# Key compression, its branch and the stick heads' projections become lanes of the attention region

## What is computed

```python
for i in range(DEPTH):                       # DEPTH = 2
    hn = rmsnorm(h, ln_mix[i])
    (g_q, g_k, g_v, g_z, g_a, g_b, n_q, n_kc, n_vc, n_ks, n_vs, n_kw, n_vw, n_gate,
     s_q, s_k, s_v) = jnp.split(hn @ w_in[i], SPLIT_POINTS, axis=-1)
    o_gdn = gated_deltanet(g_q, g_k, g_v, g_z, g_a, g_b, ...)
    o_nsa = native_sparse_attention(n_q, n_kc, n_vc, n_ks, n_vs, n_kw, n_vw, n_gate, ...)
    o_sb = stick_breaking_attention(s_q, s_k, s_v)
    mix = jnp.concatenate([o_gdn, head_rmsnorm(o_nsa), head_rmsnorm(o_sb)], axis=-1)
    h = h + mix @ w_out[i]
    ...

def compress(kv, pe, w1, w2):                # key compression: 31 blocks of 32 tokens, stride 16
    blocks = kv[:, idx] + pe[None, None, :, None, :]
    return jax.nn.silu(blocks.reshape(b, n_cmp, g, CMP_LEN * d) @ w1) @ w2

# in native_sparse_attention: three branches, each a softmax and a product, gated and added
p_c = masked_softmax(q @ kc, ...);  o_c = p_c @ vc          # the compressed branch
out = gate0 * o_c + gate1 * o_s + gate2 * o_w               # selected and window branches
```

## Time and profile before

| | us |
|---|---|
| median of 3 runs | 4019.28 |
| lowest and highest | 4017.68 and 4022.88 |
| the profiled execution | 4020.51 |
| its span | 4018.7 |

### The profile page before, as it was taken

How to read it: one execution, slowest core, us unless ns; L and a number is a source line. 1 busy time by engine, 2 the same in 40 slices (tenths; PEclk the granted TensorE clock), 3 DMA queues, 4 the chain that set the end, 5 groups by cost and what they waited for, 6 DMA issues and landing times. The chain is left out here.

```text
span 4018.7 us, 46953 instructions
## 1 busy us (share of the span) xinstructions
PE 3640.0 (91%) x19533; PEld 2787.1 (69%) x19533; DVE 1795.1 (45%) x2763; ACT 1312.1 (33%) x2028; POOL 423.9 (11%) x347
## 2 busy tenths in 40 slices
PE   5989888999998899998897979999989978799998
PEld 4777756888685668876675537788766654477885
DVE  4775556433324343325442434454454424345534
ACT  3332453222323332324222433333342124333423
POOL 0002001210001012000230000310002300003100
PEclk7999999999998899998996959999999969699999
DMA  6641324522220212303100011323131000123230
GB/s 227 205 147 37 87 69 139 173 94 90 84 79 16 104 66 94 112 32 112 40 12 23 1 54 62 110 85 116 37 98 39 12 22 1 68 74 105 78 119 23
DMA packets 230400, 316.19 MB, mean 79 GB/s; under 512 B 13085, under 2 KB 169606, under 8 KB 228910
## 3 DMA queue, kind: packets, MB, share of 16 engines
q1 hardware_dynamic: 230190, 313.20, 23.7%
HBM read 310.52 MB, written 6.85 MB: 79 GB/s over the span
## 5 line engine op out<-in xcount | busy, mean ns | idle before, releaser
L493 PE MATMUL out<-h_lo,w_hi 128*128 128x512 f32 x2608 | 1043.3, 400 | 43.9 <-DVE w_lo L484 39.7
L484 DVE TENSOR_TENSOR w_lo<-ring,w_hi 128x1024 fp32r<-128x1024 f32 (+2 forms) x473 | 582.3, 1237 | 993.8 <-ACT w_hi L479 988.9
L494 PE MATMUL out<-h_hi,w_hi 128*128 128x512 f32 x2608 | 1022.5, 392 | 0.0
L495 PE MATMUL out<-h_hi,w_lo 128*128 128x512 f32 x2608 | 1022.3, 392 | 0.0
L479 ACT ACTIVATE w_hi<-ring 128x1024 fp32r<-128x1024 f32 (+2 forms) x473 | 483.3, 1028 | 1172.4 <-PE out L495 1078.7
L493 PEld LDWEIGHTS out<-h_lo,w_hi 128*128 128x128 f32 x2608 | 494.2, 189 | 168.1 <-issue 51.0
L494 PEld LDWEIGHTS out<-h_hi,w_hi 128*128 128x128 f32 x2608 | 494.1, 189 | 112.4 <-issue 11.0
L495 PEld LDWEIGHTS out<-h_hi,w_lo 128*128 128x128 f32 x2608 | 493.8, 189 | 104.2
L493 PE MATMUL item_banks<-h_lo,w_hi 128*128 128x512 f32 (+1 forms) x696 | 317.5, 456 | 14.4 <-DVE w_lo L484 5.1
L495 PE MATMUL item_banks<-h_hi,w_lo 128*128 128x512 f32 (+1 forms) x696 | 279.4, 401 | 0.0
L494 PE MATMUL item_banks<-h_hi,w_hi 128*128 128x512 f32 (+1 forms) x696 | 279.2, 401 | 0.0
(11 more groups left out here) (487 smaller groups left out, 4654.8 us busy)
## 6 DMA issues: line engine op xcount, KB each, us to landing
ring<-in_mlp_w SPq DMA_DIRECT2D x30, 2048.0 KB, 8.7
ring<-in_w_up SPq DMA_DIRECT2D x44, 1024.0 KB, 6.5
tiles<-in_mod_w SPq DMA_DIRECT2D x80, 512.0 KB, 4.5
ring<-in_e_w_in SPq DMA_DIRECT2D x48, 512.0 KB, 4.2
ring<-in_w_in SPq DMA_DIRECT2D x22, 1024.0 KB, 5.3
ring<-in_w_down SPq DMA_DIRECT2D x10, 2048.0 KB, 7.8
ring<-in_o_w_in SPq DMA_DIRECT2D x7, 2048.0 KB, 7.9
tiles<-in_mod_w SPq DMA_DIRECT2D x8, 1024.0 KB, 8.7
```

What stands on the lines that cost most here:

```text
L484: return nc.vector.tensor_tensor(lo.bitcast(F32R), x, hi, ALU.subtract)
L493: nc.tensor.matmul(out, wh, xl, start=start, stop=False, **kw)
L494: nc.tensor.matmul(out, wh, xh, start=False, stop=False, **kw)
L495: return nc.tensor.matmul(out, wl, xh, start=False, stop=stop, **kw)
```

## The change

Three things move in each layer, and nothing that is computed changes.

- `compress_keys` and its block with its barrier go. `compress_lane` does the same work in the attention region. Its position term no longer has 32 matmuls of its own: POOL copies the vectors behind the token pairs, so that each of the 32 matmuls has 65 columns and the last column is that term. The tokens of the odd blocks between the two groups come out too and are left unused. The pairs lie in the sparse and stick tiles of `mixT`, which are empty by then.
- The compressed branch leaves the sparse lane and becomes `compressed_lane`, in the PSUM bank `stick_out`. It writes its result to `mixT` by ACT, and the sparse lane adds its own to that (`leave`). The sparse lane keeps its 48 steps in their order.
- The six items of the stick heads leave the mixing region (23 are left there) and run as an `items_lane` of the attention region, in `stick_banks`. The ring and `w1` share their memory with the stick lane's tiles, so the stick lane starts behind them. `h_hi` and `h_lo` are kept for it.

In planned times the six items take 4 to 73, the stick heads 75 to 157, the norms 159 to 208, and the sparse lane 2 to 198. In the mixing region an item beside the delta lane is planned at 9.4 where it had 8.6, and the rotary lane begins behind the last item.

```diff
-def compress_keys(k, a, l, k2, v2, kc_dup, vc_rows):
...
+def compress_lane(k, r, lane, a, l, k2, v2, w1, pairs_of, kc_dup, vc_rows, bank):
...
+    @lane.gpsimd
+    def _(pool):
+        yield 0.0
+        for i, (x, pe_at) in enumerate(((k2, V_PEK), (v2, V_PEV))):
+            if i:
+                pool.wait_ge(shifted, 5)
             for g in range(G):
...
+            nc.gpsimd.tensor_copy(pairs_of[:, i, G * S:G * S + 2 * M:2], k.vec2[:, pe_at:pe_at + M]).then_inc(shifted, 1)
+
+    @lane.tensor
+    def _(pe):
+        for i, landed in ((0, k_in), (1, v_in)):
+            for m in range(M):
+                yield 9.0 + 6.0 * i + 0.35 * m
+                if m == 0:
+                    pe.wait_ge(landed, 16)
+                    pe.wait_ge(shifted, 5 * i + 5)
+                last = nc.tensor.matmul(hid_ps[i], w1[:, i, m, :], pairs_of[:, i, 2 * m:2 * m + CMP_STRIDE * (COLUMNS - 1) + 1:CMP_STRIDE],
+                                        start=(m == 0), stop=(m == M - 1))
+        last.then_inc(hid_done, 1)
+        yield 26.0
+        pe.wait_ge(act_done, 2)
...
+def compressed_lane(k, r, lane, nq, kc_dup, vc_rows, gates, bank, kv_out, mixT):
...
+        for u in range(2):
+            yield 29.5 + 4.5 * u
...
+        for t in range(T):
+            for u in range(2):
+                yield 53.0 + 7.5 * t + 2.5 * u
...
-def sparse_lane(k, r, lane, nq, ks2, kw2, vs_rows, vw_rows, kc_dup, vc_rows, gates, mixT, tile_out):
+def sparse_lane(k, r, lane, nq, ks2, kw2, vs_rows, vw_rows, cmp_out, gates, mixT, tile_out):
...
+        def leave(t):
+            dve.wait_ge(cmp_out, t + 1)
+            dve.wait_ge(pv_done, PER_TILE * (t + 1))
+            nc.vector.tensor_tensor(mixT[:, GDN_T + t, :], mixT[:, GDN_T + t, :], out_ps[:, :], ALU.add).then_inc(tile_out, 1)
...
+        ranges = [[(W_SQ + t * P, P)] for t in range(2 * SB_T)] + [[(W_SV + t * P, P)] for t in range(2)]
+        items = [Item("feat", j, 0, P, sq[:, j, :], scale=HD ** -0.5) for j in range(SB_T)]
+        items += [Item("feat", SB_T + j, 0, P, sk[:, j, :]) for j in range(SB_T)]
+        items += [Item("rows", 2 * SB_T, 0, 2 * P, sv_rows[:, c:c + 2, :], (c, c + 1)) for c in (0, 2)]
+        at = 4.0
...
+            item.begin, item.length = at, 11.0
+            at += item.length
+
+        freed, _, item_done = items_lane(k, r, r.lane(0.0, 1.0), w, ranges, items, None, ring, w_hi, w_lo, stick_banks, quick=True)
...
-        sparse = r.lane(0.0, 100.0)
-        stick = r.lane(0.0, 60.0)
-        norms = r.lane(64.0, 42.0)
+        sparse = r.lane(2.0, 196.0)
+        stick = r.lane(at + 2.0, 82.0)
+        norms = r.lane(at + 86.0, 49.0)
...
-        items += [Item("rows", 11, 0, 2 * P, sv_rows[:, c:c + 2, :], (c, c + 1)) for c in (0, 2)]
-        items += [Item("feat", 12, j * P, P, sq[:, j, :], scale=HD ** -0.5) for j in range(SB_T)]
-        items += [Item("feat", 13, j * P, P, sk[:, j, :]) for j in range(SB_T)]
...
-            item.begin, item.length = at, 3.2 if item.load == 0 else 5.6 if at < DELTA else 8.6
+            item.begin, item.length = at, 3.2 if item.load == 0 else 5.6 if at < DELTA else 9.4
...
-            rotary_lane(k, r, r.lane(items[last_kv].begin + 1.0, 28.0), ...
+            rotary_lane(k, r, r.lane(at + 1.0, 28.0), ...
...
-            compress_keys(k, a, l, kc2, vc2, kc_dup, vc_rows)
-            attention_region(k, nq, ks2, kw2, vs_rows, vw_rows, kc_dup, vc_rows, gates, sq, sk, sv_rows, gz, mixT)
+        attention_region(k, a, l, nq, kc2, vc2, ks2, kw2, vs_rows, vw_rows, gates, sq, sk, sv_rows, gz, mixT)
```

More of the change, by code:

```diff
@@ new lines, in _ @@
+    @lane.tensor
[11 more added lines that the diff above has]
+        pe.wait_ge(act_done, 2)
+        pe.wait_ge(w2_in, 48)
+        nc.tensor.matmul(kc_ps, w2[:, 0:2, :], hid[:, 0, :], start=True, stop=True)
+        for g in range(G):
+            last = nc.tensor.matmul(vc_ps[:, g * HD:(g + 1) * HD], hid[:, 1, g * N_CMP:(g + 1) * N_CMP], w2[:, 2, :], start=True, stop=True)
+        last.then_inc(out_done, 1)
@@ new lines, in _ @@
+    @lane.vector
+    def _(dve):
+        yield 20.8
+        dve.wait_ge(hid_done, 1)
+        for i in range(2):
+            step = nc.vector.tensor_copy(pe_cols[:, i:i + 1], hid_ps[i][:, COLUMNS - 1:COLUMNS])
+        step.then_inc(pe_out, 1)
+        yield 27.5
+        dve.wait_ge(out_done, 1)
+        nc.vector.tensor_copy(kc_dup[:, :], kc_ps)
+        nc.vector.tensor_copy(vc_rows[0:N_CMP, :, :], by_group(vc_ps)).then_inc(kv_out, 1)
+    @lane.scalar
+    def _(act):
+        yield 22.0
+        act.wait_ge(pe_out, 1)
+        for i in range(2):
+            nc.scalar.activation(by_group(hid[:, i, :]), by_group(hid_ps[i][:, 0:COLUMNS - 1])[:, :, 0:N_CMP], ACT.Silu,
+                                 bias=pe_cols[:, i:i + 1]).then_inc(act_done, 1)
@@ L2772, in _ @@
             yield share(n + 1)
[L2773 to L2777 removed]
+            if n and n % PER_TILE == 0:
+                leave(t - 1)
+        leave(T - 1)
     @lane.scalar
@@ L2839, in score @@
                                  start=True, stop=True).then_inc(z_done, 1)
+        yield share(-0.56)
+        for wait in items_out:
+            pe.wait_ge(*wait)
         yield from score(0)
@@ L2989, in attention_region @@
             (mixT[:, j, :], k.vec2[:, gains[j]:gains[j] + 1], gz[:, j, :] if j < GDN_T else None,
-             (tile_out, j - GDN_T + 1) if GDN_T <= j < GDN_T + NSA_T else None) for j in order], 1.0 / HD, stick_banks, (head_out, N_SB))
-        @opening.scalar
+             (tile_out, j - GDN_T + 1) if GDN_T <= j < GDN_T + NSA_T else None) for j in order], 1.0 / HD, stick_banks, (head_out, N_SB),
+            space)
+        gate = r.lane(22.5, 1.0)
+        @gate.scalar
         def _(act):
```

310 lines of the change are left out of this document (159 added, 151 removed).

## The result

| | us | ratio to before (95% interval) |
|---|---|---|
| before, median | 4020.28 | |
| changed kernel, median of 4 | 3977.72 (3970.35 to 3991.06) | 0.9898 (0.987 to 0.9925) |
| the same code in a second session | 3995.16 (3990.09 to 3999.37) | 0.9935 (0.9922 to 0.9947) |
| in a third | 3999.86 (3995.7 to 4001.62) | 0.9947 (0.993 to 0.9964) |
| forecast | 3931 (3868 to 3990) | |

The change is faster, by 42.6 us where it was first timed and by 22 to 27 in two later sessions; the forecast was 88. Before stayed within 4013 to 4029 in every session, so the spread is the changed kernel's own.

The account below looks back on a forecast made before the run. PE bounds the delta rounds, compression runs alone at half clock, and the chain from scores to scaled probabilities limits attention. Per layer -41.0 - 31 + 28 = -44, twice -88: 3932.5, or 3931 us at the median; range 3868 to 3990.

Parts of the forecast that it names:

- compression block: Separate compression block before the attention region, barrier included: disappears, -41.0 us a layer.
- mixing region: Delta rounds lose six items: -31 us a layer, between -24 and -38; round 4 becomes 33 us.
- opening: Start of the attention region: PE idles some 7.5 us while the items' first weights land and are split.
- beside the items: Attention region, items with compression, compressed branch and 18 sparse steps: 89 us, between 78 and 100.
- beside the stick heads: Attention region, stick heads with 18 sparse steps instead of 28: 86 us against 109.6, between 76 and 98.
- end: Attention region, last 12 sparse steps and 8 norms: 61 us against 59.2, between 46 and 65.
- Clock: near 1.0 beside the items: Expected sign in the attention region: PE's clock near 1.0 beside items, about 0.9 beside stick heads, 0.6 at the end.
- rival D: Attention region: PE's clock stays low after the opening's wait, +122 us on the parts, 4175 us; chance 0.05.
- Edits at nothing: Attention region: addition in `leave`, the gates' Silu with table loads, and the stick lane's wait for banks add no time.
- C: Attention region: ACT and DVE steps block each other, items keep mixing-region cost; +60 us, 4001; chance 0.18 for 3957 to 4010.
- A: The forecast itself, all terms as summed: 3931 us, own range 3905 to 3957; chance 0.50.
- B: Attention region swallows the moved work in its waits, staying 215.5 us: 3869 us; chance 0.25 for 3857 to 3905.

Follow-up runs that it names:

- the filler there: Changed kernel with 24 extra matmuls of 512 columns, read by nothing, on PE in the opening ahead of the first item: 3981.13 us, ratio 0.9905.
- the compression half alone: Changed kernel with the six items back in the mixing region: 3980.99 us (0.9902); with two extra matmuls ahead of every sparse step's transposes, 3980.18 (0.9903).

## Why the prediction was wrong

The first median, 3977.7, lies inside the range of 3868 to 3990, the two later ones outside; the gains are 43, 27 and 22 us for 88. By its own terms, for a layer, forecast against the profile of 3991.06, whose miss is 12 us larger than the first median's:

| term | forecast | layer 0, layer 1 |
|---|---|---|
| compression block | -41.0 | -41.0, -40.9 |
| mixing region | -31 | -30, -29 |
| opening | 7.5 | 8.6, 8.6 |
| beside the items | 89 (78 to 100) | 102.3, 109.2 |
| beside the stick heads | 86 (76 to 98) | 104.5, 104.4 |
| end | 61 (46 to 65) | 55.4, 55.4 |

- **Compression and mixing** held. Round 4 took 34.0 us for 33, round 3 41.3 for 40. That 17 of the 41 us are the shorter code and need no lane, the forecast did not say.
- **Beside the stick heads** is the first step that failed, by 18 us: "Ten steps fewer at 2.44 give 85". The step of the earlier trace rows is one of four blocks, and those that left were 8, not 10, with 18 blocks together. At the 0.7 that the runs gave, they are worth 13 us, not 24; that is 11 of the 18. In the part beside the items I had myself used 1.35 for a mean step. Another 5 is the clock, 0.84 there for before's 0.91, which I had put at about 0.9. The rest, 1 to 2 us, may be the first scores, which before lay in the prologue.
- **Beside the items** is the second step that failed, by 13 and 20 us. The work was sized well: 94 us without low clock, by the lengths above, for 89. The other 8 and 15 us are the lower level. "Clock: near 1.0 beside the items" was argued from the delta rounds, dense and behind dense work; this stretch stands behind an opening of 8.6 us with PE idle for most of it, and the filler there showed that the idle time brings the low clock behind it, 9 and 26 us. The mechanism stood in the text as rival D, but as all or nothing: held for the whole region it makes the kernel slower, so it got 0.05, and none of it went into the sum. It holds for 18 to 46 us a layer.
- **End.** 55.4 us for 61, at 0.75 where 0.6 was expected, and with 10 steps in it instead of 12.
- **Edits at nothing.** POOL's copies cost next to nothing: the first split in the opening took 1.59 us beside them for 1.23, as the exclusive lock of the Trainium skill (SBUF — State Buffer, section SBUF: two separate sides) would have it. With compression back in a block of its own that split took 1.23, and the opening 7.1 and 6.5 us for 8.6. So the compression's copies and loads together cost some 2 us of the opening, and the 4.9 did not appear.
- **The rivals.** C came nearest: 3966 was the border between A and C, and all medians lie above. Its reason was partly right (every block kept its price); its 110 beside the items had the right size by the wrong cause, changes of work instead of the clock. B fell: the rule that weight loads, not busy time, show PE's headroom (the Trainium skill, Perfetto Trace Analysis, section Identifying the Most-Contended Engine) agrees with the trace here: at 46.6% beside the heads PE took two filler matmuls a step more, and the stretch still fell from 104.5 to 101.3 us. But the headroom was of no use to the steps, whose transposes wait for DVE's scaling, at a fixed place in PE's list.

## What to carry to other kernels

Price a step that is moved by its own size, not by the one that stands in a row nearby, and count what is moved in units of work (blocks of keys) rather than in steps. Two chains of waits in fixed order on the same engines may add up to the full sum of both: put one alone once, and subtract. Where a change both shortens the code of a piece and moves it, time the shorter code in its old place first; here that may be most of the gain. Where a wait is put ahead of dense PE work, charge a part of that work at the lower clock in the sum itself, not only as a rival. And run the kernel compared with in every session: its median moved by 22 us between sessions while before moved by 2.

## What was not expected

The same instructions took 98, 102, 109 or 114 us, by how long PE's granted clock stayed at its lower level, and the same lengths came back in other sessions. Useless matmuls in PE's waits made the changed kernel some 30 us faster (0.9863 and 0.9873 for 0.9935 and 0.9947), before 6 us, and the compression half alone not at all. The idle opening explains the lower level right behind it; what makes PE fall to that level further on, in stretches whose program is the same, stays open.
